# Sums of squares of the q and k heads as two float32r products, with the low parts made on GpSimd and VectorE

## The chip, the cores and the metric

The kernel runs on one core of one Trainium2 chip. Its time is the device time of one execution in microseconds (us); the median of several runs is compared. The engines are named as in the profile: PE is TensorE's matmul, PEld its weight load, DVE is VectorE, ACT is ScalarE, POOL is GpSimd, and SP issues most of the transfers.

## The reference

The reference computes two transformer blocks over 512 tokens of width 1024. The part that the change touches is in the first block, a gated DeltaNet with four heads of 128:

```
qkv = jax.nn.silu(centred_depthwise_conv(jnp.concatenate([q, k, v], axis=-1), conv_w))
q, k, v = jnp.split(qkv.astype(jnp.float32), 3, axis=-1)
q = l2_norm(q.reshape(b, s, DN_HEADS, DN_HEAD_DIM)) * (DN_HEAD_DIM ** -0.5)
k = l2_norm(k.reshape(b, s, DN_HEADS, DN_HEAD_DIM))

def l2_norm(x):
    return x * lax.rsqrt(jnp.sum(x * x, axis=-1, keepdims=True) + EPS)
```

There are eight such heads, four of q and four of k. Around them stand the input projection (`h @ w_in`), a second attention with rotary embedding in the same block, and the recurrence that uses the normed q and k.

## The kernel before

**Storage.** q and k lie with the 128 channels of a head on the partitions: `QK[:, j, :]` is head j (0 to 3 are q, 4 to 7 are k) by 512 tokens, in float32. A sum over a head's channels is thus a sum over partitions. It is made on PE by a product with a 128x128 matrix of ones, whose result holds the sum in every partition.

**Precision of the large products.** Each weight and each activation is split into a high part in float32r and a low part, and a product is three float32r products (high by high, high by low, low by high; `mm3`). A unit of weights is loaded by SP into `RAW`, ACT writes its high part `WH` (`prep`), and POOL writes the low part `WL = RAW - WH` (`prep`, 128x1024). Four buffers of each go round. In rows of the trace the high and low parts are `wh`, `wl` and `xh`, `xl`.

**Order of work.** Every engine has one queue and runs it strictly in order. One list, ORDER, is built at the top of the program by calls of `do(name, ...)`; each engine walks the list and emits its own part of every step, so a step's place in the list is its place in each queue. Waits are semaphores: `mark.up(key)` counts, `on.wait_ge(*mark.at(key))` waits. The eight PSUM banks are handed out by rings (`G.take`); whoever takes a bank waits on PE for its last reader.

**The stretch around the change.** Twelve units j = 0 to 11 of the projection give q, k and v by channel. For each, PE makes 24 products (`ch`), DVE multiplies the bank by the token's norm (`conv_rms`; rows `bank<-bank,rb`), ACT copies it with the middle tap (`conv_copy`), DVE adds the other four taps with four instructions (`conv`; rows `qk<-bank,pparams,qk`, and `vc<-...` for j of 8 and more), and ACT applies SiLU (`silu`). One step behind follows ACT's square of a finished head (`square`, into `SL8[j]`). Between these stand DVE's steps for gates and for the rotary embedding (`gate_beta`, `rope(3)` in step 2, `gate2` in step 4, `rope_k` in step 6), and POOL's weight preparations.

Then 16 pieces of a token-wise projection (`tok_pieces`, six products each; rows `bank<-wh,xh` and so on) run on PE. Behind pieces 3, 4, 5 and 6 PE makes two sums of squares each (`qsum`), from the ring of banks 6, 7, 5, 4. ACT takes the logarithm of each sum (`sl<-bank,ceps`), later the exponential of -0.5 times it, and DVE multiplies the head by the result (`qk<-qk,sl`). The sums' banks 4 and 5 were last used by `conv` 10 and `conv` 11. After that come the matrix inversions of the recurrence and the windowed attention, then the rest of both blocks.

Of the kernel before, what the change touches and what calls it, by code (L numbers as in the profile page):

```python
# [7 lines left out]
F32 = mybir.dt.float32  # L8
F32R = mybir.dt.float32r
BF16 = mybir.dt.bfloat16  # L10
ALU = mybir.AluOpType
# [186 lines left out]
def program(nc, x, xt, wflat, cfd, ppd, prd, wsd, tbd, seld, out):  # L198
# [58 lines left out]
    VT = zb("vt", [128, 4, 512], F32, 80)  # L257
    SL8 = [zb(f"sl{j}", [128, 512], F32, 72 + 2 * j) for j in range(8)]
    MIX = zb("mix", [128, 4, 1024], F32, 88)
    SWR = zb("swr", [128, 4, 640], F32, 104)  # L260
# [114 lines left out]
    def mark(name):  # L375
        marks.append(Mark(nc, name))
        return marks[-1]
# [5 lines left out]
    conv_a, conv_v, conv_s = mark("conv_a"), mark("conv_v"), mark("conv_s")  # L383
    qk_p, qk_a, qk_v = mark("qk_p"), mark("qk_a"), mark("qk_v")
    tok_p, tok_a = mark("tok_p"), mark("tok_a")
# [259 lines left out]

    G.over((6, 7, 5, 4))
    for n in tok_pieces(U_SZ, "sz"):
        if 3 <= n < 9:
            step(g1, 2)
# [488 lines left out]
    def pool_engine(e):  # L1138
# [12 lines left out]
        def prep_half(k):  # L1151
# [3 lines left out]
                w_lo.up(0 if k else "first"), 1)  # L1155

        def inv_mb(cb, d):
            W = WORK[cb]
            mb = W["MB"][d][:]
            on.wait_ge(*inv_v.at(("mb0", cb, d)))  # L1160
            e.tensor_tensor(h3(mb), h3(mb), bc4((cf("SL"), cf("SU"))[d]), ALU.mult).then_inc(inv_g.up(("mb1", cb, d)), 1)  # L1161
            if d:
                on.wait_ge(*inv_g.at(("mb1", cb, 1)))
                both = W["MB"][0][:]
                e.tensor_tensor(both, both, mb, ALU.add).then_inc(inv_g.up(("mb", cb)), 1)  # L1165
# [109 lines left out]
        def finish(tb):  # L1275
            if tb == 3:
# [3 lines left out]

        return dict(finish=finish, prep=prep, prep_half=prep_half, inv_mb=inv_mb, inv_m=inv_m, inv_mt=inv_first, inv_d=inv_d, inv_tri=inv_tri, inv_x7=inv_x7, inv_causal=inv_causal, z_gain=z_gain, swa_o=swa_o,
                    vb_first=vb_first, scan_vb=scan_vb, scan_kd=scan_kd, gm_w=gm_w, gm_sq=gm_sq, gm_gain=gm_gain, fa_norm=fa_norm, fa_low=fa_low)
# [3 lines left out]
    def scalar_engine(e):  # L1286
# [69 lines left out]
        def square(j):  # L1356
            on.wait_ge(*conv_s.at(j))
            on.wait_ge(*rope_v.at(("ss", 3) if j < 4 else "ssk"))
            act(SL8[j][:], QK[:, j, :], ACT.Square, qk_a.up(("sq", j)))

# [294 lines left out]
    def vector_engine(e):  # L1655
# [35 lines left out]
        def masks():  # L1691
# [6 lines left out]
            e.tensor_copy(IDb[:], cf("ident")).then_inc(const_set.up("id"), 1)  # L1698
            ts(HALF[:], cf("ident"), 0.5, None, ALU.mult, const_set.up("half"))
            e.memset(LNQ[:], -0.5 * math.log(128.0)).then_inc(const_set.up("lnq"), 1)  # L1700
            on.wait_ge(s_params, 32)
# [8 lines left out]
        def conv(j):  # L1710
# [3 lines left out]
            for n, i in enumerate((0, 1, 3, 4)):  # L1714
                lo, hi, sh = max(0, 2 - i), min(T, T + 2 - i), i - 2
                if n:
                    on.wait_ge(*conv_v.at((j, n)))
                stt(dst[:, lo:hi], psum[b][:, lo + sh:hi + sh], pp("dn_conv_w", j * 5 + i), dst[:, lo:hi], ALU.mult, ALU.add,
                    conv_v.up((j, n + 1)))

        def qexp(j):
# [416 lines left out]
        def finish(tb):  # L2138
# [12 lines left out]
            for n in range(tb // 3, 2):  # L2151
                c = slice(n * 512, (n + 1) * 512)
                stt(OUT[:, tb, c], H[:, tb, c], rr, GAIN[:, c], ALU.mult, ALU.mult, fin_v.up(("out", tb, n)))

        return dict(begin=begin, x_split=x_split, conv_rms=conv_rms, scale=scale, split=split, masks=masks, conv=conv, qexp=qexp, gate_dt=gate_dt, gate_beta=gate_beta, gate2=gate2, rope_tables=rope_tables, rope_sq=rope_sq,
                    rope_root=rope_root, rope=rope, rope_keys=rope_keys, rope_k=rope_k, rope_t=rope_t, inv_decay=inv_decay, inv_mb=inv_mb, inv_q=inv_q, inv_m=inv_m,
# [7 lines left out]
    def tensor_engine(e):  # L2164
# [147 lines left out]
        def qsum(j):  # L2312
            p = bank(("qsum", j))
            on.wait_ge(s_const, 16)
            on.wait_ge(*qk_a.at(("sq", j)))
            mm(p[:, :], cf("ones"), SL8[j][:], True, True).then_inc(qk_p.up(j), 1)

# [359 lines left out]
```

## Time and profile before

| | |
|---|---|
| median of 3 runs | 923.9 us (923.84 to 924.92) |
| the profiled execution's own time | 923.39 us |
| its span, first to last instruction | 921.6 us |
| PE busy | 906.2 us, 98% of the span |
| DVE busy | 481.8 us, 52% |
| ACT busy | 457.4 us, 50% |
| POOL busy | 464.1 us, 50% |
| mean granted TensorE clock | 0.999 |

Busy time is an average over stages with different limits. Matmuls are pipelined, so the duration of a PE row (0.39 us for 128x512) is longer than the distance between the starts of two, and it is the distance that counts in a sum. A float32 product appears as two PE instructions. Names in rows are out<-in, with buffer numbers left out: `sl` is any of the eight `SL8`.

### The profile page before, as it was taken

The page shows a single profiled execution, that of the slowest core. Times are in us where ns is not written, and L with a number is a line of the kernel's source. Part 1 is how long each engine was busy: PE and PEld are TensorE (multiplying, and loading weights), DVE is VectorE, ACT ScalarE, POOL GpSimd, SP SyncE. Part 2 cuts the span into 40 slices and gives each one's busy share as a digit, 9 for nine tenths or more (in the row PEclk, how much of TensorE's full clock was granted, in tenths as well). Part 3 has the DMA queues.
Part 4 walks back from the last instruction along what each step waited for, and adds up shares of the span by engine and source line. Part 5 has one row for each costly group of instructions (what it writes and reads, how often), then busy time and mean ns, then how long its engine had stood idle before and what let it go on. Part 6 is the DMA issues. An engine that isn't in the chain of part 4 may idle for free.

```text
span 921.6 us, 11979 instructions
## 1 busy us (share of the span) xinstructions
PE 906.2 (98%) x4752; PEld 763.7 (83%) x4752; DVE 481.8 (52%) x814; ACT 457.4 (50%) x817; POOL 464.1 (50%) x262
## 2 busy tenths in 40 slices
PE   9999999999999999999999999999999999999997
PEld 6988868899999888788777889888888888888885
DVE  4679836898857443533654434333333334654434
ACT  6666587576546444447557245333343433433223
POOL 4453432987566433456786426444444444344440
PEclk9999999999999999999999999999999999999999
DMA  9522310000022714332221214233222233232202
GB/s 344 191 91 91 97 42 1 1 1 2 2 92 68 267 46 137 115 92 70 75 86 46 97 60 132 101 104 101 92 92 92 91 96 110 73 133 93 91 23 92
DMA packets 25303, 83.63 MB, mean 91 GB/s; under 512 B 3008, under 2 KB 3264, under 8 KB 25120
## 3 DMA queue, kind: packets, MB, share of 16 engines
q1 hardware_dynamic: 24240, 81.49, 26.4%
q10 hardware_dynamic: 1008, 1.38, 0.4%
q8 instruction: 38, 0.62, 0.3%
q14 instruction: 17, 0.14, 0.0%
HBM read 78.66 MB, written 2.10 MB: 88 GB/s over the span
## 4 chain that ended last, share of the span: by engine, by line
PE 81%; DVE 9%; POOL 5%; ACT 3%; DMA 1%; issue 1%; SPq 0%; DVEq 0%; ACTq 0%
PE bank L2168 78%; PE bank L2176 3%; DVE qk L1665 2%; DVE vc L1665 1%; POOL mb L1161 1%; POOL wl L1149 1%; DVE r L1659 1%; ACT L1290 1%; DMA xt<-in_xt 1%; POOL mb L1165 1%; POOL p L1251 1%; POOL dd L1171 1%; DVE bank L1659 0%; ACT vc L1290 0%; ACT xh L1290 0%
## 5 line engine op out<-in xcount | busy, mean ns | idle before, releaser
L1149 POOL TENSOR_TENSOR wl<-raw,wh 128x1024 fp32r<-128x1024 f32 (+1 forms) x129 | 310.3, 2410 | 364.0 <-ACT wh L1290 364.0
L2168 PE MATMUL bank<-xh,wh 128*128 128x512 f32 (+1 forms) x536 | 206.8, 386 | 0.0
L2168 PE MATMUL bank<-xl,wh 128*128 128x512 f32 (+1 forms) x536 | 205.2, 383 | 0.0
L2168 PE MATMUL bank<-xh,wl 128*128 128x512 f32 (+1 forms) x528 | 202.2, 383 | 0.0
L1290 ACT ACTIVATE wh<-raw 128x1024 fp32r<-128x1024 f32 (+2 forms) x132 | 136.0, 1035 | 123.9 <-PE bank L2168 117.8
L2168 PE MATMUL bank<-wh,xh 128*128 128x512 f32 (+1 forms) x352 | 140.5, 399 | 0.8 <-POOL wl L1149 0.4
L2168 PE MATMUL bank<-wh,xl 128*128 128x512 f32 (+1 forms) x352 | 134.5, 382 | 0.0
L2168 PE MATMUL bank<-wl,xh 128*128 128x512 f32 (+1 forms) x352 | 134.1, 381 | 0.0
L2168 PEld LDWEIGHTS bank<-xh,wh 128*128 128x128 f32 x536 | 100.8, 188 | 19.3 <-issue 0.2
L2168 PEld LDWEIGHTS bank<-xl,wh 128*128 128x128 f32 x536 | 100.8, 188 | 19.2
L2168 PEld LDWEIGHTS bank<-xh,wl 128*128 128x128 f32 x528 | 99.2, 188 | 19.6
L2168 PEld LDWEIGHTS bank<-wh,xh 128*128 128x128 f32 x352 | 66.3, 188 | 15.5 <-POOL wl L1154 1.7
L1659 DVE TENSOR_TENSOR al<-ac,ah 128x512 fp32r<-128x512 f32 x22 | 53.6, 2450 | 45.8 <-ACT ah L1290 45.8
L2168 PEld LDWEIGHTS bank<-wh,xl 128*128 128x128 f32 x352 | 66.1, 188 | 13.0
L2168 PEld LDWEIGHTS bank<-wl,xh 128*128 128x128 f32 x352 | 66.4, 189 | 11.8 <-issue 1.0
L1665 DVE SCALAR_TENSOR_TENSOR ta<-bank,pparams,ta 128x510 f32<-128x510 f32 (+1 forms) x44 | 32.9, 749 | 74.1 <-ACT ta L1290 73.3
L2168 PE MATMUL bank<-wh,ah 128*128 128x512 f32 x176 | 68.5, 389 | 0.0
L2168 PE MATMUL bank<-wl,ah 128*128 128x512 f32 x176 | 68.5, 389 | 0.0
L2168 PE MATMUL bank<-wh,al 128*128 128x512 f32 x176 | 68.5, 389 | 0.0
L1665 DVE SCALAR_TENSOR_TENSOR tgg<-bank,pparams,tgg 128x510 f32<-128x510 f32 (+1 forms) x44 | 33.0, 749 | 62.4 <-ACT tgg L1290 61.6
L1290 ACT ACTIVATE tgg<-bank,pparams 128x512 f32<-128x512 f32 x22 | 17.2, 781 | 78.8 <-PE bank L2168 78.8
L1251 POOL TENSOR_SCALAR p<-p,dn 128x512 f32<-128x512 f32 (+3 forms) x32 | 34.8, 1089 | 16.8 <-DVE dn L2079 16.7
(271 smaller groups left out, 1424.7 us busy)
## 6 DMA issues: line engine op xcount, KB each, us to landing
raw<-in_wflat SPq DMA_DIRECT2D x126, 512.0 KB, 3.5
xt<-in_xt SPq DMA_DIRECT2D x8, 256.0 KB, 4.4
h<-in_x SPq DMA_DIRECT2D x4, 512.0 KB, 8.1
h<-in_x SPq DMA_DIRECT2D x1, 2048.0 KB, 8.3
gain<-in_pr SPq DMA_DIRECT2D x3, 512.0 KB, 5.0
consts<-in_cf SPq DMA_DIRECT2D x1, 1088.0 KB, 10.5
raw<-in_wflat SPq DMA_DIRECT2D x4, 272.0 KB, 11.0
kh<-kh SPq DMA_DIRECT2D x8, 128.0 KB, 2.3
```

The costliest lines, as they stand in the source:

```text
L1149: e.tensor_tensor(WL[u % NS][:, 0:n], RAW[u % NS][:, 0:n], WH[u % NS][:, 0:n].bitcast(F32), ALU.subtract).then_inc(w_lo.up(u), 1)
L1161: e.tensor_tensor(h3(mb), h3(mb), bc4((cf("SL"), cf("SU"))[d]), ALU.mult).then_inc(inv_g.up(("mb1", cb, d)), 1)
L1165: e.tensor_tensor(both, both, mb, ALU.add).then_inc(inv_g.up(("mb", cb)), 1)
L1171: e.tensor_tensor(h3(W["DD"][:, lower(d)]), h3(raw(cb)), bc4(cf("LM", d)), ALU.mult).then_inc(inv_g.up(("dd", cb, 0, d)), 1)
L1251: e.tensor_scalar(p, p, DN2[:, qb, h:h + 1], None, ALU.mult).then_inc(fa_g.up(n), 1)
L1290: return e.activation(out_, in_, f, **k).then_inc(up, 1)
L1659: return e.tensor_tensor(out_, a, b, op).then_inc(up, 1)
L1665: return e.scalar_tensor_tensor(out_, a, s, b, op0, op1).then_inc(up, 1)
L2168: return e.matmul(o, l, r_, start=start, stop=stop, skip_group_check=part)
L2176: return e.transpose(o, in_, cf("ident")[0:in_.shape[0], 0:in_.shape[0]])
```

## The change

1. POOL gets a step `square`: it computes head squared in float32 into `SL8[j]`, at the place in the list where ACT has its square.
2. ACT's square now writes float32r into a new tile `SQH[j]`: the high part.
3. DVE gets a step `sq_low`: `SQL[j] = SL8[j] - SQH[j]`, float32r, in the place of `SL8[j]`. The eight stand behind `conv` 11.
4. PE's `qsum` makes two float32r products with a float32r matrix of ones (`ONES`, made once by DVE), high then low, in place of one float32 product.
5. The ring of banks for the sums is 6, 7, 4, 5.

```
-    G.over((6, 7, 5, 4))
+    G.over((6, 7, 4, 5))
     for n in tok_pieces(U_SZ, "sz"):
+        if n < 4:
+            do("sq_low", 2 * n)
+            do("sq_low", 2 * n + 1)
         if 3 <= n < 9:
             step(g1, 2)
...
+        def square(j):
+            on.wait_ge(*conv_s.at(j))
+            on.wait_ge(*rope_v.at(("ss", 3) if j < 4 else "ssk"))
+            e.tensor_tensor(SL8[j][:], QK[:, j, :], QK[:, j, :], ALU.mult).then_inc(qk_g.up(j), 1)
...
-            act(SL8[j][:], QK[:, j, :], ACT.Square, qk_a.up(("sq", j)))
+            act(SQH[j][:], QK[:, j, :], ACT.Square, qk_a.up(("sq", j)))
...
+            ts(ONES[:], cf("ones"), 1.0, None, ALU.mult, const_set.up("ones"))
...
+        def sq_low(j):
+            on.wait_ge(*qk_a.at(("sq", j)))
+            on.wait_ge(*qk_g.at(j))
+            tt(SQL[j][:], SL8[j][:], SQH[j][:].bitcast(F32), ALU.subtract, sq_v.up(j))
...
+            on.wait_ge(*const_set.at("ones"))
             on.wait_ge(*qk_a.at(("sq", j)))
-            mm(p[:, :], cf("ones"), SL8[j][:], True, True).then_inc(qk_p.up(j), 1)
+            mm(p[:, :], ONES[:], SQH[j][:], True, False)
+            on.wait_ge(*sq_v.at(j))
+            mm(p[:, :], ONES[:], SQL[j][:], False, True).then_inc(qk_p.up(j), 1)
```

On PE, behind piece 3 of the token-wise projection, before (the first and the second pair of sums, six products of piece 4 between them):

```order
L2168 MATMUL bank6<-sl0_79,consts_61 128x512 [waits qk_a,s_const,gate_v]
L2168 MATMUL bank7<-sl1_80,consts_61 128x512 [waits qk_a]
...
L2168 MATMUL bank5<-sl2_81,consts_61 128x512 [waits qk_a,conv_v]
L2168 MATMUL bank4<-sl3_82,consts_61 128x512 [waits qk_a]
```

The same place on PE in the changed kernel:

```order
L2186 MATMUL bank6<-sqh0_87,onesr_95 128x512 [waits const_set,qk_a,s_const,gate_v]
L2186 MATMUL bank6<-sql0_96,onesr_95 128x512 [waits sq_v]
L2186 MATMUL bank7<-sqh1_88,onesr_95 128x512 [waits qk_a]
L2186 MATMUL bank7<-sql1_97,onesr_95 128x512 [waits sq_v]
...
L2186 MATMUL bank4<-sqh2_89,onesr_95 128x512 [waits qk_a,conv_v]
L2186 MATMUL bank4<-sql2_98,onesr_95 128x512 [waits sq_v]
L2186 MATMUL bank5<-sqh3_90,onesr_95 128x512 [waits qk_a,conv_v]
```

Every sum now has two products, and the second of them waits for a result of DVE (`sq_v`), in the first pair too.

On DVE, the end of the twelfth unit's taps and what stands behind it in the changed kernel:

```order
L1677 SCALAR_TENSOR_TENSOR vc_76<-bank5,pparams_62,vc_76 128x510 [waits conv_v]
L1671 TENSOR_TENSOR sql0_96<-sl0_79,sqh0_87 128x512 [waits qk_g,qk_a]
L1671 TENSOR_TENSOR sql1_97<-sl1_80,sqh1_88 128x512 [waits qk_g,qk_a]
L1671 TENSOR_TENSOR sql2_98<-sl2_81,sqh2_89 128x512 [waits qk_g,qk_a]
```

Before, the last tap of `vc` was followed directly by `qk<-qk,sl`; now the eight subtractions stand between the two, and none stands ahead of the taps.

On POOL, the weight preparations of steps 2 to 6, in the changed kernel:

```order
L1156 TENSOR_TENSOR wl1_58<-raw1_50,wh1_54 128x1024 [waits w_hi]
L1167 TENSOR_TENSOR sl0_79<-qk_75 128x512 [waits rope_v,conv_s]
L1156 TENSOR_TENSOR wl2_59<-raw2_51,wh2_55 128x1024 [waits w_hi]
L1167 TENSOR_TENSOR sl1_80<-qk_75 128x512 [waits conv_s]
L1156 TENSOR_TENSOR wl3_60<-raw3_52,wh3_56 128x1024 [waits w_hi]
L1167 TENSOR_TENSOR sl2_81<-qk_75 128x512 [waits conv_s]
L1156 TENSOR_TENSOR wl0_57<-raw0_49,wh0_53 128x1024 [waits w_hi]
L1167 TENSOR_TENSOR sl3_82<-qk_75 128x512 [waits conv_s]
L1156 TENSOR_TENSOR wl1_58<-raw1_50,wh1_54 128x1024 [waits w_hi]
L1167 TENSOR_TENSOR sl4_83<-qk_75 128x512 [waits rope_v,conv_s]
L1156 TENSOR_TENSOR wl2_59<-raw2_51,wh2_55 128x1024 [waits w_hi]
L1167 TENSOR_TENSOR sl5_84<-qk_75 128x512 [waits conv_s]
```

Before, only the `wl` rows stood there; one square has been put behind each of eight preparations (two more follow those shown).

## Rows read from the trace of the kernel before

**Rows 1.** Busy by stretch: PE, PEld, DVE, ACT, POOL, then granted clock, DMA share, GB/s.
```profile
60.00:108.60 48.60, 48.60 (x219) 40.29 (x218) 44.93 (x66) 28.38 (x41) 20.99 (x9) 1.00 0.26 90
108.60:127.30 18.70, 18.17 (x66) 12.02 (x65) 7.44 (x11) 11.93 (x17) 5.82 (x3) 1.00 0.21 68
```
**Rows 2.** The chain in order of time, 90 to 320 us: start, duration, engine.
```profile
117.82 21.83 PE bank L2168 x84
```
**Rows 3.** Timeline of PE, 103 to 128 us: start, duration, engine, instruction [idle before].
```profile
103.14 0.39 PE L2168 MATMUL bank<-xh,wh 128*128 128x512 f32 x1
...
113.79 0.39 PE L2168 MATMUL bank<-wh,xl 128*128 128x512 f32 x1
114.02 1.88 PE L2168 MATMUL bank<-sl,consts 128*128 128x512 f32 x4
...
117.82 1.98 PE L2168 MATMUL bank<-sl,consts 128*128 128x512 f32 x4 [0.53 <-DVE vc L1665]
...
121.02 1.88 PE L2168 MATMUL bank<-sl,consts 128*128 128x512 f32 x4
...
127.22 0.40 PE L2168 MATMUL bank<-wh,xh 128*128 128x512 f32 x1
```
**Rows 4.** Timeline of DVE, 129 to 135 us.
```profile
129.75 5.17 DVE L1659 TENSOR_TENSOR qk<-qk,sl 128x512 f32<-128x512 f32 x8 [11.98 <-ACT sl L1290]
```
**Rows 5.** Timeline of ACT, 118 to 120 us.
```profile
118.45 1.28 ACT L1290 ACT_TABLE_LOAD   x1
```
**Rows 6.** Tile `vsq`: shortest, median and longest ns of POOL's square of a tile.
```profile
L1268 POOL TENSOR_TENSOR vsq<-vg x4: 1035/1043/1062, 434.1 to 450.7; 128x512 f32<-128x512 f32 x4
```
**Rows 7.** Timelines of POOL and of DVE, 62 to 71 us.
```profile
62.42 2.40 POOL L1149 TENSOR_TENSOR wl<-raw,wh 128x1024 fp32r<-128x1024 f32 x1 [4.58 <-ACT wh L1290]
66.41 2.50 POOL L1149 TENSOR_TENSOR wl<-raw,wh 128x1024 fp32r<-128x1024 f32 x1 [1.59 <-ACT wh L1290]
...
62.71 2.14 DVE L1662 TENSOR_SCALAR beta<-beta 128x32 f32<-128x32 f32 x1
...
65.80 0.26 DVE L1665 SCALAR_TENSOR_TENSOR gg<-spa,ea 128x16 f32<-128x16 f32 x2
...
66.70 3.43 DVE L1659 TENSOR_TENSOR r<-swr,turnq 128x512 f32<-128x512 f32 x3
```
**Rows 8.** Timelines of POOL (86 to 102 us) and of DVE (80 to 94 us).
```profile
86.85 2.41 POOL L1149 TENSOR_TENSOR wl<-raw,wh 128x1024 fp32r<-128x1024 f32 x1 [2.38 <-ACT wh L1290]
90.46 2.67 POOL L1149 TENSOR_TENSOR wl<-raw,wh 128x1024 fp32r<-128x1024 f32 x1 [1.19 <-ACT wh L1290]
99.96 2.42 POOL L1149 TENSOR_TENSOR wl<-raw,wh 128x1024 fp32r<-128x1024 f32 x1 [6.83 <-ACT wh L1290]
...
80.83 0.19 DVE L1659 TENSOR_TENSOR nbeg<-nbeta,eg 128x32 f32<-128x32 f32 x1 [1.61 <-ACT eg L1290]
...
88.39 1.42 DVE L1659 TENSOR_TENSOR swr<-swr,ssk 128x512 f32<-128x512 f32 x1
89.85 3.56 DVE L1659 TENSOR_TENSOR r<-swr,turnk 128x512 f32<-128x512 f32 x3
```
**Rows 9.** Timelines of POOL and of DVE, 162 to 166 us.
```profile
162.40 1.30 POOL L1161 TENSOR_TENSOR mb<-mb,consts 128x512 f32<-128x512 f32 x1
163.65 1.75 POOL L1210 TENSOR_TENSOR ds<-ds,consts 128x512 f32<-128x512 f32 x1
...
163.16 1.09 DVE L1659 TENSOR_TENSOR mb<-ee,nbeta 128x512 f32<-128x512 f32 x1
```
**Rows 10.** Busy by stretch at the end of the span, columns as in rows 1.
```profile
914.00:916.00 2.00, 1.49 (x7) 0.91 (x5) 0.77 (x2) 0.72 (x2) 1.29 (x1) 1.00 0.66 246
...
918.00:919.00 1.00, 0.00 (x0) 0.00 (x0) 0.47 (x1) 0.50 (x1) 0.00 (x0) 0.93 0.00 0
919.00:920.00 1.00, 0.00 (x0) 0.00 (x0) 0.00 (x0) 0.00 (x0) 0.00 (x0) 0.50 0.66 252
```
**Rows 11.** Timeline of PE, 0 to 12 us: the program's first products.
```profile
1.47 5.49 PE L2168 MATMUL bank<-zero 128*128 128x512 f32 x6 [1.47 <-DVE zero L1669]
```

More of the change, by code:

```diff
@@ L258, in program @@
     SL8 = [zb(f"sl{j}", [128, 512], F32, 72 + 2 * j) for j in range(8)]
+    SQH = [zb(f"sqh{j}", [128, 512], F32R, 32 + 2 * j) for j in range(8)]
+    ONES = sb("onesr", [128, 128], F32R, small_at[0])
+    small_at[0] += 0.5
+    SQL = [zb(f"sql{j}", [128, 512], F32R, 72 + 2 * j) for j in range(8)]
     MIX = zb("mix", [128, 4, 1024], F32, 88)
@@ L383, in program @@
     conv_a, conv_v, conv_s = mark("conv_a"), mark("conv_v"), mark("conv_s")
-    qk_p, qk_a, qk_v = mark("qk_p"), mark("qk_a"), mark("qk_v")
+    qk_p, qk_a, qk_v, qk_g, sq_v = mark("qk_p"), mark("qk_a"), mark("qk_v"), mark("qk_g"), mark("sq_v")
     tok_p, tok_a = mark("tok_p"), mark("tok_a")
@@ L1279, in finish @@
                 e.tensor_tensor(HG[:], H[:, 3, 0:512], GAIN[:, 0:512], ALU.mult).then_inc(fin_g.up("hg"), 1)
-        return dict(finish=finish, prep=prep, prep_half=prep_half, inv_mb=inv_mb, inv_m=inv_m, inv_mt=inv_first, inv_d=inv_d, inv_tri=inv_tri, inv_x7=inv_x7, inv_causal=inv_causal, z_gain=z_gain, swa_o=swa_o,
+        return dict(finish=finish, square=square, prep=prep, prep_half=prep_half, inv_mb=inv_mb, inv_m=inv_m, inv_mt=inv_first, inv_d=inv_d, inv_tri=inv_tri, inv_x7=inv_x7, inv_causal=inv_causal, z_gain=z_gain, swa_o=swa_o,
                     vb_first=vb_first, scan_vb=scan_vb, scan_kd=scan_kd, gm_w=gm_w, gm_sq=gm_sq, gm_gain=gm_gain, fa_norm=fa_norm, fa_low=fa_low)
@@ L2153, in finish @@
                 stt(OUT[:, tb, c], H[:, tb, c], rr, GAIN[:, c], ALU.mult, ALU.mult, fin_v.up(("out", tb, n)))
-        return dict(begin=begin, x_split=x_split, conv_rms=conv_rms, scale=scale, split=split, masks=masks, conv=conv, qexp=qexp, gate_dt=gate_dt, gate_beta=gate_beta, gate2=gate2, rope_tables=rope_tables, rope_sq=rope_sq,
+        return dict(begin=begin, x_split=x_split, conv_rms=conv_rms, scale=scale, split=split, masks=masks, conv=conv, sq_low=sq_low, qexp=qexp, gate_dt=gate_dt, gate_beta=gate_beta, gate2=gate2, rope_tables=rope_tables, rope_sq=rope_sq,
                     rope_root=rope_root, rope=rope, rope_keys=rope_keys, rope_k=rope_k, rope_t=rope_t, inv_decay=inv_decay, inv_mb=inv_mb, inv_q=inv_q, inv_m=inv_m,
```

## The prediction

> **What bounds the kernel now.** I read the stretches first, then the chain in order of time, then the timelines of the engines on both sides of the change. From 60 to 108.6 us PE is never idle, but DVE is busy for 44.93 of 48.60 us [rows 1]: two engines run side by side there, and busy shares do not say which one is late. The chain of work does. Through the units 2 to 11 it lies on DVE (taps, gates, rotary embedding), with short turns to ACT, up to the last tap of `conv` 11. At 117.82 it passes to PE, which then holds it for 21.83 us without a gap [rows 2]. So PE, though busy, has slack ahead of 117.8: it starts unit 11 at 103.14 and is at the first pair of sums at 114.02 [rows 3], almost 4 us before DVE is through. It stands still once only, 0.53 us in front of the second pair, for bank 5 and its reader `conv` 11 [rows 3]. **Whatever delays DVE between 62 and 118 us delays the end by as much, and whatever PE must await from DVE behind `conv` 11 is on the path.** The change does both.
>
> **The products.** Forty-eight products start between 103.14 and 114.02, the last at 113.79, so one float32r product costs 10.65/47 = 0.227 us [rows 3]. From 121.02 to 127.22 there are two pairs of float32 sums and twelve products: 6.20 us, less 12 x 0.227, leaves 1.74 us a pair [rows 3]. A pair in the new form is four float32r products, 0.91 us. Four pairs save 4 x 0.83 = 3.3 us of PE work, and the new order of banks would let the first of the second pair go ahead of `conv` 11. No row shows float32r products with a matrix of ones, but only the values differ.
>
> The Trainium skill (TensorE: Matmul & The Clock Gate, Back-to-back issue gap) gives 131 ns for a sustained 512-column product in a stream with weight loads. By that figure a new pair would cost 0.52 us as an estimate, and the three pairs behind the first wait would end 1.2 us earlier. The rows show 0.227 us in just such a stream, and I go by them.
>
> **The wait that the change adds.** The low product of the first sum waits for `sq_low` 0, and DVE reaches `sq_low` only behind `conv` 11. Before, ACT's squares had been made long ahead. The nearest row to one subtraction is DVE's `qk<-qk,sl`, of the same size and also with two SBUF inputs: 8 in 5.17 us, so 0.65 each, 0.60 where they follow each other closely [rows 4]. With `conv` 11 ending at 117.8 (PE starts at 117.82, released by it [rows 3]), the first low part is there at 118.45 and the second at 119.05. PE then does the last product of pair 1 (0.23), six products (1.36), and three times a pair and six products (0.91 + 1.36 = 2.27): 119.07 + 0.23 + 1.36 + 6.80 = 127.46. Before, the same point is 127.22 [rows 3]. **The whole saving is thus used up, +0.24 us.** The later low parts come every 0.60 us against 0.91 us for two sums and 1.36 us between pairs, so only the first pair waits. Queued behind PE's wait are all later products; all of them wait. ACT does not add to it: its table load ends at 119.73 [rows 5], when the first two sums are done.
>
> **The squares on POOL.** Eight more instructions. The nearest row is POOL's own square of a 128x512 tile, 1.043 us [rows 6]; POOL's products of two tiles of that size take 1.30 us [rows 9], which is the upper bound. POOL itself is only 43% busy there [rows 1], and a square by itself delays no weights that matter. But the rows show that a VectorE instruction with SBUF inputs cannot run during a POOL instruction: `beta`, 128x32, takes 2.14 us from 62.71 until POOL's 62.42 + 2.40 is over; `swr<-swr,ssk` takes 1.42 instead of 0.69; three `r` take 3.43 and 3.56 us around POOL's other preparations [rows 7, 8]. The taps, which read PSUM, keep their length. And the turn goes to whoever waits when an instruction ends: `mb<-ee,nbeta` on DVE gets in between two POOL instructions, and the second of these takes 1.75 us where its like takes 1.30 [rows 9].
>
> With that I go through DVE's queue.
> - *62 to 71 us (`gate_beta`, `rope(3)`).* Square 0 stands directly behind the preparation that ends at 64.82, so `nbeta` waits until about 65.87, 0.6 us late. Then `gg`, at 65.80 before, comes after 66.41, when the next preparation holds the port, and it and `swr` (0.6 us) no longer fit in ahead of it. They run from 68.85 on. Square 1, ready behind that preparation, takes one more turn of 1.04 us. Sum: 0.6 to 0.9 us for the order, plus 1.04: **1.6 to 1.9 us** later.
> - *78 us (`gate2`).* Square 2 can delay `ngc` by a turn, but DVE waits 1.61 us for ACT right there [rows 8]. Nothing.
> - *88 to 94 us (`rope_k`).* Four `swr`/`r` steps and the sum `swr` stand against two preparations [rows 8]. Now POOL has preparation, square 4, preparation, square 5 without a gap, as the heads 4 and 5 are finished one step earlier. Each square gets one turn between DVE's instructions: **2 x 1.04 = 2.0 us** (2.1, less what the two overlap between instructions).
> - Squares 3, 6 and 7 fall beside taps. Nothing.
>
> Sum 3.5 to 3.9 us; I take 3.8. At the upper price of 1.30 a square it would be 4.6, at none of it 0. The same squares made at the rate that the Trainium skill gives for GpSimd's `tensor_tensor` (GPSIMD Engine Reference, Elementwise — side-by-side cycle accounting), about 2.6 cycles an element, would be an estimate of 1.11 us each and 4.0 us in all.
>
> Behind 94 us DVE's chain has no slack, so `conv` 11 ends at 121.6. PE's slack takes a part: the weights of unit 11 are ready at 99.96 + 2.42 = 102.38 [rows 8], only 0.76 us ahead of their use, and ACT's preparation follows DVE. So PE stands 3.0 us in front of unit 11, arrives at pair 1 at 117.1, and waits there from 117.3 to 122.2. That costs nothing more, since it is waiting for the same DVE.
>
> **Small parts.** DVE's `ONES` is one 128x128 instruction in the opening stretch, where PE's products bind; at most 0.2 us. The new addresses cost nothing. The subtractions use DVE's idle 11.98 us [rows 4].
>
> **Sum.** 0.24 + 3.8 = +4.0 us on a span of 921.6 us. The profiled execution took 923.39 us and would take 927.4; the median of the runs is 0.5 us above it. **Forecast 928.0 us.** Behind 127 us everything hangs on PE's piece stream [rows 2], so I see no slack that gives a part back.
>
> **Rivals.**
> 1. *The clock falls during the long wait.* Before, PE is busy for 48.60 of 48.60 and 18.17 of 18.70 us here, with the clock at 1.00 [rows 1]. At the end of the span its last products end at 915.5, and the granted clock falls to 0.50 (1.2 GHz) inside 918 to 919 [rows 10]. The wait from 117.3 to 122.2 is longer than that. At the start, PE works at the low level from 1.47 to about 7 us: three float32 products take 5.49 us, 1.83 each [rows 11] against 0.87 above. If the clock falls and comes back after a similar time, some 5.5 us at half speed lose about 2.7 us: 930.7 us. For it: the length. Against it: the wait could be 1 us shorter if DVE loses less. The Trainium skill (TensorE: Matmul & The Clock Gate, What's actually happening) has the chip look at the activity in windows that run on regardless of the kernel, so a wait of this length would sometimes be caught and sometimes not, in the runs of one kernel; no row before can show this.
> 2. *The squares pass beside DVE* (another turn order, or a square that is not kept out). Then only the +0.24 remains: 924.1 us, with part of the loss up to 925.7.
> 3. *Faster.* The wait at pair 1 would have to be gone: then 3.3 us and the stall of about 0.7 us (0.53 in the row, and the restart) are saved, 919.9 us. It decides itself by whether `sq_low` 0 is done when PE arrives at 114.2; it stands behind `conv` 11 in DVE's queue, so DVE would have to end its taps 4 us earlier. The change takes nothing from DVE ahead of that point. A weaker form: the delay of PE is caught up further on, where the inversions keep ACT, DVE and POOL busy. But what starts those is PE's own stream.
>
> **How the numbers follow.** Forecast mechanism, clock kept: 0.45. With the clock falling: 0.27. Little or no loss on DVE (924.1 to 925.7): 0.13. A part of the loss (925.8 to 926.8): 0.08. Faster: 0.05. Above 932: 0.02. The range leaves out the faster case and the lower half of the case without loss below, and the last above: 925.0 to 932.0. By itself the forecast mechanism spans 926.9 to 928.8. A difference of 0.2%, 1.8 us, is about what a measurement of this kernel tells from none; slower by more is 0.45 + 0.27 + 0.08 + 0.02 and a little of the third case, 0.83; within it 0.12; faster 0.05.
>
> **What would show each step.** In the timeline of PE: sums as pairs of float32r products 0.227 us apart, a wait for DVE's `sql` in front of the first low product, of 4 to 5 us, and none at the other pairs. On DVE: `nbeta` or `gg` near 66 us and the `r` near 90 us stretched further, the last tap at about 121.6, first `sql` directly behind it. On POOL: squares of 1.04 us. In the stretches: a clock below 1.00 behind 121 us or not. The prediction is wrong if the last tap still ends near 118, if PE does not stop at pair 1, or if the piece stream behind the sums does not set the next stage's start.

## The result

The changed kernel takes 928.5 us in the median of five runs (927.29 to 930.51), the kernel before, timed beside it, 924.92 us: a ratio of 1.0045, interval 1.0032 to 1.0058. It is slower by 0.45%. Its profiled execution took 930.51 us, with a span of 928.7 us, against 923.39 us and 921.6 us.

The chain of work in order of time (start, duration, what), around the change. It answers to [rows 2].

```profile
67.54 4.29 DVE r L1671 x3
...
91.55 5.14 DVE r L1671 x3
...
121.69 23.21 PE bank L2186 x93
```

As before, DVE holds the chain up to the last tap and then PE takes it over, but at 121.69 and no longer at 117.82. The timeline of PE (start, duration, engine, instruction, idle before); it answers to [rows 3].

```profile
105.74 0.47 PE L2186 MATMUL bank<-xh,wh 128*128 128x512 f32 x1 [2.01 <-POOL wl L1156]
...
116.74 0.40 PE L2186 MATMUL bank<-sqh,onesr 128*128 128x512 f32 x1
...
121.69 0.50 PE L2186 MATMUL bank<-sql,onesr 128*128 128x512 f32 x1 [4.54 <-DVE sql L1671]
...
122.29 0.75 PE L2186 MATMUL bank<-sql,onesr 128*128 128x512 f32 x1
...
127.89 0.39 PE L2186 MATMUL bank<-sqh,onesr 128*128 128x512 f32 x1
...
128.58 0.40 PE L2186 MATMUL bank<-sql,onesr 128*128 128x512 f32 x1
```

The reader sees the sums as float32r products, 0.23 us apart in the third pair (127.89 to 128.58), and one wait of 4.54 us in front of the very first low product. The second low product takes 0.75 us. Why, the stretches of PE tell (busy, then granted clock):

```profile
120.00:122.00 2.00, 0.31 (x1) 1.00 0.00 0
122.00:124.00 2.00, 2.00 (x6) 0.59 0.00 0
124.00:126.00 2.00, 2.00 (x6) 0.55 0.00 0
126.00:128.00 2.00, 2.00 (x10) 1.00 0.00 0
```

TensorE comes back from the wait and drops to its lower level, 1.2 GHz, for 3.4 us; in that time products start 0.43 us apart instead of 0.23. Before, the clock was 1.00 throughout here [rows 1]. What keeps DVE late is in its own timeline and POOL's; they answer to [rows 7, 8, 4].

```profile
63.15 2.15 DVE L1674 TENSOR_SCALAR beta<-beta 128x32 f32<-128x32 f32 x1
65.33 0.35 DVE L1758 RECIPROCAL beta<-beta 128x32 f32<-128x32 f32 x1
65.72 0.58 DVE L1674 TENSOR_SCALAR nbeta<-beta 128x32 f32<-128x32 f32 x1
...
67.54 4.28 DVE L1671 TENSOR_TENSOR r<-swr,turnq 128x512 f32<-128x512 f32 x3
...
91.55 5.13 DVE L1671 TENSOR_TENSOR r<-swr,turnk 128x512 f32<-128x512 f32 x3
...
117.93 3.10 DVE L1677 SCALAR_TENSOR_TENSOR vc<-bank,pparams,vc 128x510 f32<-128x510 f32 x4 [0.76 <-ACT vc L1302]
120.95 4.89 DVE L1671 TENSOR_TENSOR sql<-sl,sqh 128x512 fp32r<-128x512 f32 x8
```

And POOL's:

```profile
65.22 1.04 POOL L1167 TENSOR_TENSOR sl<-qk 128x512 f32<-128x512 f32 x1
66.85 2.92 POOL L1156 TENSOR_TENSOR wl<-raw,wh 128x1024 fp32r<-128x1024 f32 x1 [0.58 <-ACT wh L1302]
69.72 1.49 POOL L1167 TENSOR_TENSOR sl<-qk 128x512 f32<-128x512 f32 x1
...
90.93 1.49 POOL L1167 TENSOR_TENSOR sl<-qk 128x512 f32<-128x512 f32 x1
92.38 2.84 POOL L1156 TENSOR_TENSOR wl<-raw,wh 128x1024 fp32r<-128x1024 f32 x1
95.18 1.22 POOL L1167 TENSOR_TENSOR sl<-qk 128x512 f32<-128x512 f32 x1
```

The three `r` that took 3.43 us take 4.28, those that took 3.56 take 5.13, with POOL's squares beside them; the squares take 1.04 us by themselves, as in [rows 6], and up to 1.49 where DVE has a turn first. The last tap ends at about 120.95, and the eight `sql` follow at 0.60 us each.

**Where the 7.1 us of span lie.** I compare the start of each TensorE product with that of the same product before. The shift is 0.41 us already at 13.4 us, in the opening, where the kernels hardly differ; other kernels' executions have it too, and it is not the change's. Behind the last pair of sums it is 5.28 us; below, "the end of the sums" is always the same product, the second behind the last pair (126.07 us before). DVE's own start in this stretch is 0.44 us late at 62.71 us (63.15). It loses 1.26 us more by 72 us and another 1.57 by 97 us, 2.83 together, and the last taps start 3.27 us late. With 0.24 for the pairs and 1.7 for the clock (the products of the 3.4 us started at about half the rate) that makes 0.44 + 2.83 + 0.24 + 1.7 = 5.2 of the 5.28 us. A last step, 1.7 us, comes at 195 us, far from the change. There DVE adds the sinks of the attention to its maxima, a tile of 128x8 (`es`). First its row, then POOL's beside it:

```profile
198.34 3.03 DVE L1671 TENSOR_TENSOR es<-rparams,mx 128x8 f32<-128x8 f32 x1
```
```profile
196.33 5.02 POOL L1200 TENSOR_TENSOR mp<-ds,consts 128x512 f32<-128x512 f32 x4
```

In the kernel before the same instruction, with the same four `mp` beside it, took 0.54 us. The experiments show that this step belongs to neither kernel.

The granted clock of the whole execution is known for the other timed runs too. It was 0.998 in the profiled execution, with its 3.4 us at the lower level, and 0.995 to 0.997 in the other four. No profiled execution on record in which the clock fell only at the very end of the span has less than 0.998. So the clock very probably fell in those four as well.

### The profile page after: what moved, and what is told of

Read it like the earlier page. It is cut to its first block, busy times and chain, and to the rows that moved or that the text cites. A ratio compares the mean times of both kernels' runs of the same rounds, so it can differ in the third digit from the quotient of the medians.

```text
span 928.7 us, 12007 instructions
## 1 busy us (share of the span) xinstructions
PE 905.0 (97%) x4752; PEld 764.7 (82%) x4752; DVE 493.7 (53%) x823; ACT 457.8 (49%) x817; POOL 474.0 (51%) x270
## 4 chain that ended last, share of the span: by engine, by line
PE 79%; DVE 11%; POOL 5%; ACT 3%; issue 1%; DMA 1%; SPq 0%; DVEq 0%; ACTq 0%
PE bank L2186 76%; PE bank L2194 3%; DVE qk L1677 2%; DVE vc L1677 1%; DVE r L1671 1%; POOL mb L1173 1%; POOL wl L1156 1%; DVE dt L1671 1%; ACT L1302 1%; DMA xt<-in_xt 1%; POOL mb L1177 1%; POOL p L1263 1%; POOL dd L1183 1%; DVE bank L1671 0%; ACT vc L1302 0%
```

## The experiments

Each kernel was timed in five rounds beside the kernel before. "Shift" is always the start of TensorE's products against the profiled execution of the kernel before, and holds the opening's part where nothing else is said: 0.2 to 0.5 us, and -0.2 us in experiment 6.

**1. The squares out of DVE's way.** POOL makes them while DVE reads PSUM.

```
         if 2 <= j <= 9:
             do("square", j - 2)
+        for i in {5: (0, 1), 7: (2, 3, 4, 5, 6), 8: (7,)}.get(j, ()):
+            do("square_low", i)
```
(`square` is ACT's alone now, `square_low` POOL's; from head 2 on it also waits for the end of `rope_k`.)

> The change, with POOL's squares moved to where DVE runs only taps that read PSUM: two in step 5, five in step 7 behind the last swr of the rotated keys, one in step 8. Everything else as changed. My account (DVE kept off its SBUF inputs by POOL's squares costs 2.85 us): the last tap of conv 11 ends 2.5 to 3 us earlier than in the changed kernel (at 117.8 to 118.2 of the span), the wait at the first pair stays at 4 us or so, and the time is 2.5 to 3 us below the changed kernel's, that is about +0.3 to +2 us against the kernel before (0.24 and what a fall of the clock costs). Rival (the squares are not what delays DVE): last tap still near 121, time still +3.5 to +4.5 us.

Measured: 927.39 us (926.36 to 928.17), ratio 1.0032 [1.002, 1.0044]; the profiled execution 926.36 us. DVE's delay is gone: no wait for `wl`, and `conv` 11 ends at 118.0. The low product is there at 118.66, but the clock falls here too. PE's timeline:

```profile
118.66 0.80 PE L2190 MATMUL bank<-sql,onesr 128*128 128x512 f32 x1 [4.03 <-DVE sql L1675]
```

Its stretches (busy, then granted clock):

```profile
116.00:118.00 2.00, 0.00 (x0) 0.72 0.33 133
118.00:120.00 2.00, 1.34 (x3) 0.50 0.00 0
120.00:122.00 2.00, 2.00 (x6) 0.50 0.00 0
122.00:124.00 2.00, 2.00 (x7) 0.58 0.00 0
```

The shift at the end of the sums is 2.86 us: 0.2 of the opening, 0.24, and about 2.5 for 5 us of products at 1.2 GHz. So the delay of DVE is one cause, and the wait for `sq_low` behind `conv` 11 is a second one that stays by itself and brings the third, the clock. The median falls by only 1.1 us, less than the 2.8 us that DVE regains. The six runs had a granted clock of 0.994 to 0.997, the changed kernel's 0.995 to 0.998, so the clock took a larger part here; the profiled execution is the fastest of the six.

**2. PE kept at work during the wait.** Eighteen discarded products, results of no use, stand between the first high and the first low product.

```
             mm(p[:, :], ONES[:], SQH[j][:], True, False)
+            if j == 0:
+                spare = bank(("qsum", 1))
+                for _ in range(18):
+                    mm(spare[:, :], XH[:, 0, 0:128], WH[0][:, 0:512], True, True)
```

> The change, with 18 products whose result is thrown away on PE behind the first high product, in a bank of a later sum, so that PE works through most of its long wait. My account (the granted clock fell to 0.5 because of that wait and cost 1.7 us): the clock stays at 1.00 around 120 us, and the time is about 1.7 us below the changed kernel's, +2 to +2.5 us against the kernel before. Rival (the fall of the clock is hidden by other waits, or was a chance of the one profiled run): time as the changed kernel's, +3.6 to +4, with the clock kept.

Measured: 928.88 us (928.07 to 929.58), ratio 1.0044 [1.0031, 1.0056]. PE's timeline, and a stretch (busy, then granted clock):

```profile
117.04 4.24 PE L2186 MATMUL bank<-wh,xh 128*128 128x512 f32 x18
121.74 0.50 PE L2186 MATMUL bank<-sql,onesr 128*128 128x512 f32 x1 [0.46 <-DVE sql L1671]
```
```profile
120.00:122.00 2.00, 1.54 (x7) 1.00 0.00 0
```

The clock stays at 1.00 in every stretch from 118 to 126 us, PE's last wait is 0.46 us, and the shift at the end of the sums is 3.85 us, 1.43 less than in the changed kernel. But `es` at 196.90 us took 3.01 us here too, and in the timed runs nothing of the gain is to be seen, although their granted clock was 0.997 to 0.999 against the changed kernel's 0.995 to 0.998. The clock's price is thus shown in the trace alone, not in the medians, and what hides it there is open.

**3. The high part taken twice.** The kernel before, with two float32r products of the high part for each sum, in the new ring, and neither squares on POOL nor `sq_low`. It leaves out the low part, and its sums are twice as large.

> The kernel before with ACT's square in float32r, two float32r products of the high part per sum, the new order of banks, no squares on POOL and no subtractions. Leaves out the low part and adds the high part twice, so the sums are twice as large. My account (the products save 0.83 us a pair, the order of banks some of the stall of 0.7): PE stands in front of conv 11's bank until 117.8, and the end of the sums comes at 124.2 in place of 127.2: 3.0 us faster than before. Rival (the saving does not reach the end, because another engine binds behind the sums): within 1 us of before.

Measured: 923.73 us (922.16 to 925.4, 11 runs), ratio 0.9985 [0.9975, 0.9995], profiled 922.62 us. A pair takes 0.93 us against the 0.91 of the estimate, so the saving of 3.3 us of PE's work is real. But at the end of the sums the shift is -1.37 us (-1.85 without the opening's part), not -3.0. The expectation missed; the list of PE's waits in the stretch says where it went (total, times, longest):

```profile
PE bank L2172 <- DVE vc L1668: 0.9, 1, 0.9
PE bank L2172 <- ACT sl L1293: 0.6, 1, 0.6
```

PE runs ahead and stands, first for the bank of `conv` 11, then at the third pair for bank 6, which ACT frees only by its first logarithm: behind `conv` 11 ACT must apply SiLU, load a table and then take the logarithm.

**4. The order of banks alone.** The kernel before with the ring 6, 7, 4, 5.

> The kernel before with the new order of banks only. My account: the first sum of the second pair (0.87 us) goes ahead of conv 11's end, the wait of 0.53 us and its restart go, 0.7 us faster than before. Rival: no difference, as DVE binds anyway.

Measured: 924.48 us (923.17 to 926.4, 11 runs), ratio 1.0001 [0.9992, 1.0011]. In the trace the wait at the second pair is gone, and from 118.35 to 120.79 us the shift is -0.34 us, 0.8 less than in the opening. Half of this goes at the third pair, which starts at 120.97 us and not at 120.69, where PE's stream would have it: as in experiment 3 it takes bank 6, and ACT reads that bank only from 120.23 on. About 0.4 us are left up to 195 us (a shift of 0.06 to 0.00 against the opening's 0.46). Then 1.7 us are lost: DVE's timelines of the kernel before (first) and of this one (second):

```profile
193.01 0.54 DVE L1659 TENSOR_TENSOR es<-rparams,mx 128x8 f32<-128x8 f32 x1
```
```profile
193.01 3.03 DVE L1659 TENSOR_TENSOR es<-rparams,mx 128x8 f32<-128x8 f32 x1
```

Both begin at 193.01, with POOL's four `mp` from 191.0 to 196.0 beside them. In the one execution DVE gets in between two of them, in the other it is passed over until the last is done. This is a difference of the execution and not of the change. It fits the times of the kernel before: of its 100 timed runs beside the changed kernel and these experiments 40 lie between 923.17 and 924.09 us, 60 between 924.81 and 927.26, and none between. The top of the upper group goes with a lower clock: of the 95 runs beside the experiments eleven have a granted clock of 0.996, and they are the eleven slowest, 926.20 to 927.26 us; all others have 0.998 or more.

**5 and 6. That small step later.** `es` and ACT's exponential of it are made one piece later, in the changed kernel and in the kernel before (DVE's part; ACT's likewise).

```
-            if h == 7:
-                on.wait_ge(*swa_v.at(("mx", n)))
-                tt(ES[:, qb, :], pr("swa_sinks"), MX[:, qb, :], ALU.add, swa_v.up(("es", qb)))
+            for m in range(n - 1, n + 1):
+                if m >= 0 and m % 8 == 7 and (m < n or n == 31):
+                    on.wait_ge(*swa_v.at(("mx", m)))
+                    tt(ES[:, m // 8, :], pr("swa_sinks"), MX[:, m // 8, :], ALU.add, swa_v.up(("es", m // 8)))
```

> The changed kernel with one small step moved: the sum of sinks and maxima (es, 128x8) of a block of attention is made one piece later, and ACT's exp of it too, so that VectorE's small operation at 198 us no longer stands beside GpSimd's row of four mp operations. Theory: that operation took 3.03 us because GpSimd held the port over several operations; moved, it takes under 1.4 us, the shift of TensorE's products against the kernel before stays at the value that it has at the end of the sums (5.3 us with the clock's fall, 3.6 without), and the timed runs lie at 926.0 to 927.5 with a spread under 1 us. Rival: the 1.7 us at 195 to 200 us come from another wait (ACT or TensorE), and come back at the same place: median 928.5.

> The same move in the kernel before. Theory: the timed runs of the kernel before fall into two groups (923.2 to 923.9 and 924.8 to 926.6) by whether the small operation meets GpSimd's row; with it moved, only the lower group is left: median 923.2 to 923.9, ratio 0.998 to 1.000, and the difference between this run and the one with the changed kernel is the change's own price: 2.85 for VectorE's delay, 0.24 for the wait, 0 or 1.7 for the clock, so 2.6 to 4.8 us. Rival: two groups stay, as the step has another cause.

Measured: 928.46 us (927.06 to 929.85) and 924.46 us (the median of eleven runs, one of them of 3230.82 us; the others 923.33 to 925.34), ratios 1.0032 [1.0022, 1.0042] and 0.9987 [0.9977, 0.9997]. In both traces the first `es` took 1.12 to 1.14 us and no step is left at 195 us (the shift of experiment 6 at its end is -0.07 us). But the spread did not fall under 1 us, and the median of experiment 6 is 924.5 us, not 923.2 to 923.9. So the theory holds in the profiled executions and is not confirmed by the times: something more spreads them, and it is not the clock, which was granted at 0.998 or more in all of experiment 6's runs. In experiment 8, which moves the step too, `es` even took 2.40 us: a later place is no sure way out. The two kernels differ by 4.0 us in the medians, inside the 2.6 to 4.8 expected for the change's own price.

The trace of experiment 5 has something else, PE's stretches at the preceding wait:

```profile
104.00:106.00 2.00, 0.34 (x2) 1.00 0.00 0
106.00:108.00 2.00, 2.00 (x8) 0.76 0.64 217
108.00:110.00 2.00, 2.00 (x6) 0.50 0.11 45
```

PE has stood for `wl` for 2.02 us, as in the changed kernel, and here the clock falls behind this wait; in the executions of the changed kernel and of experiments 8 and 10 it stayed at 1.00 behind the same wait. It fell a second time during the wait of 2.94 us for `sql`, at 120.7 us, before PE was back at 121.61. The shift at the end of the sums is 6.24 us.

**7 and 8. The sums three pieces later.** `if 6 <= n < 12` in place of `if 3 <= n < 9`, so that PE asks for the sums eighteen products later, 4.1 us at 0.227 each (the expectation of experiment 8 says 3.3); experiment 7 with the squares as in experiment 1, experiment 8 with the squares left where the change has them, both with the sinks' step moved.

> The changed kernel with the sinks' step moved, GpSimd's squares placed where VectorE reads PSUM or a bank, and the sums of squares put three pieces later in TensorE's order (pairs 0 to 5 between pieces 6 and 11 of the step instead of 3 and 8). Theory: VectorE is not held up, sq_low of the first head is there before TensorE asks for it, nothing waits, and the clock stays at 1.00: the products save 3.3 us and the kernel before's own wait of 0.53 us goes as well; 3.3 to 3.9 us under the kernel before with the sinks moved, 919.5 to 920.5. Rival 1: ACT's logarithm behind the last convolution frees the first bank late and holds part of it back, as with the high part taken twice: 921 to 922. Rival 2: the later place in the order itself costs what follows the sums (transposes, rope): 923 or more.

> As the run above, but GpSimd's squares stay where the change has them. Theory: VectorE ends the last convolution 2.85 us late, at about 120.7, TensorE has three pieces more to do before it asks (some 3.3 us of products), so its wait shrinks from 4.54 us to 1 us or less, the clock stays at 1.00, and the saving of 3.3 us is there against a delay that now lies partly beside TensorE: 920.5 to 923.5. If 2.85 us of VectorE's delay still reach the end, the rival that the delay and not the wait costs: 923 to 924.

Measured: 925.47 us (923.84 to 926.91, 11 runs), ratio 1.0003 [0.9993, 1.0013], and 929.54 us (the median of seven runs, one of them of 1833.76 us; the others 927.78 to 929.73), ratio 1.0037 [1.0023, 1.0051]. Both are slower than the theory had it. In experiment 7 the long wait is gone, the clock is 1.00, and the shift is -2.17 us once all sums are made, from 127.5 us on. Then it goes back to +0.46 at 138 us. PE's timeline, then ACT's and DVE's:

```profile
138.59 0.50 PE L2192 MATMUL bank<-wh,xh 128*128 128x512 f32 x1 [2.46 <-ACT mix L1306]
```
```profile
137.84 2.42 ACT L1306 ACTIVATE mix<-bank,rs 128x512 f32<-128x512 f32 x4
```
```profile
118.07 9.32 DVE L1676 TENSOR_TENSOR sql<-sl,sqh 128x512 fp32r<-128x512 f32 x8
```

PE needs a bank that ACT empties by `mix`, and `mix` stands in ACT's queue behind SiLU, three table loads, eight logarithms, eight exponentials and weight splits. Before, `mix` began at 136.85 and with the 0.75 us that lie between the start of `mix` and PE's product here, PE could have gone on at 137.60, while it came at 138.12. So 0.5 us is all that PE can come forward as long as ACT does not. Here ACT is itself 1 us later, for the last logarithms must wait for the last sums; and these were late because POOL's `wl` preparations, two of them at 119.85 and 123.39 us, now fall beside the eight `sql`, which take 9.32 us instead of 4.89. Experiment 8 adds to this the 2.0 us for `wl` and the delay of DVE. Behind its wait for `mix`, 2.45 us, the clock fell too (0.50 from 142 to 144 us) and took 1.6 us, which the wait of 2.46 us at the same place in experiment 7 did not bring; with 1.2 us more at `es` it ends at +6.22 us. Rival 2 of the expectation came about. Rival 1 did not: no sum of experiment 7 waited for a bank, and PE's waits there were for `sql` (0.67 us) and for `mix`.

**9 to 11. Three low parts early.** In front of the taps of `conv` 9, 10 and 11 DVE waits 0.76 us for ACT's copy. Experiment 9 makes one `sql` in each of these gaps, and has the squares as in experiment 1.

```
+        if j >= 9:
+            do("sq_low", j - 9)
...
-            do("sq_low", 2 * n)
-            do("sq_low", 2 * n + 1)
+        for i in (2 * n, 2 * n + 1):
+            if 3 <= i < 8:
+                do("sq_low", i)
```

> The changed kernel with GpSimd's squares out of VectorE's way and the first three low parts (sql of heads 0 to 2) made in VectorE's gaps of 0.76 us in front of the taps of convolutions 9, 10 and 11, where it waits for ACT's vc. Theory: TensorE's first low products find their operands, the wait for sql (4.0 us without this step) falls under 0.5 us and the clock stays at 1.00 between 112 and 130 us; the products are 3.3 us shorter and TensorE's old wait of 0.53 goes, but ACT (silu, table load, eight logarithms, exponentials, copies to mix) has only 1.1 us of idle time between 117.8 and 139 us in the kernel before and becomes the bound, so TensorE waits for ACT's sl or mix and only 1.0 to 1.7 us are left at the end: profiled execution 922.0 to 922.8 when the small operation at 195 us is short, ratio 0.998 to 0.999. Rival: ACT is no bound, the whole 3.3 to 3.8 us reach the end: 919.5 to 920.0, ratio 0.996.

Measured: 923.63 us (922.6 to 926.66, 12 runs), ratio 0.9991 [0.9981, 1.0001]; profiled 922.99 us. The first low product no longer waits, the clock stays at 1.00, and the shift at the end is -0.42 us, the opening's 0.4 included. ACT's timeline:

```profile
118.75 0.63 ACT L1308 ACTIVATE vc<-vc 128x512 f32<-128x512 f32 x1 [3.17 <-DVE vc L1683]
119.40 1.28 ACT L1308 ACT_TABLE_LOAD   x1
120.70 2.42 ACT L1308 ACTIVATE sl<-bank,ceps 128x512 f32<-128x512 f32 x4
...
123.94 2.44 ACT L1308 ACTIVATE sl<-bank,ceps 128x512 f32<-128x512 f32 x4
...
136.50 2.43 ACT L1308 ACTIVATE mix<-bank,rs 128x512 f32<-128x512 f32 x4
```
PE's one longer wait is 1.4 us, for the bank of `conv` 11. From SiLU to `mix` ACT now has no gap: 17.75 us, against 19.05 before, which had 1.08 us of waiting for PE. So of the 3.3 us saved on PE about 1.3 us can reach `mix`, and 0.95 us of this is lost again, as SiLU starts at 118.75 instead of 117.80: 0.24 stem from before 104 us, the rest from the `sql` before `conv` 9. That one took 1.65 us, for a `wl` (103.81 to 106.21) ran beside it. DVE's timeline:

```profile
105.12 1.65 DVE L1677 TENSOR_TENSOR sql<-sl,sqh 128x512 fp32r<-128x512 f32 x1
```

Experiment 10 has the three early low parts, with the squares left where the change has them.

> The changed kernel with the three early low parts alone; GpSimd's squares stay where the change has them. Theory: VectorE still ends convolution 11 some 2.85 us late (about 120.6 to 121), ACT's silu and the logarithms start that much later, and TensorE waits for a bank or for convolution 11 instead of for sql; with ACT as the bound behind it, nearly the whole 2.85 us less the 1.1 of ACT's idle time reach the end: shift at the end +1.5 to +3.0 against the kernel before, plus what the clock costs where the wait is over 2 us: 925.5 to 928. Rival: the delay mattered only through the wait for sql, which is gone: 923 or less.

Measured: 927.0 us (926.1 to 927.78, 11 runs), ratio 1.0022 [1.0013, 1.0031]. The shift behind the sums, at 142 us, is 2.52 us against -0.38 in experiment 9: **the squares' place costs 2.9 us**, with the clock at 1.00 in both profiled executions and nothing else different up to there; the medians differ by 3.4 us. The timed runs are less clean: seven of the eleven here have a granted clock of 0.996 or 0.997, in experiment 9 three of twelve. Those seven are no slower than the other four, so the difference of the medians is not the clock's. The rival, that the delay mattered only through the wait for `sql`, is out.

Experiment 11 was to move one weight split out of ACT's row.

```
     do("conv", 11)
+    w_ahead(U_SZ + 2)
     do("silu", 11)
```

> As the first run of this batch, and one weight split (wh of the third unit of the projection beside the sums, 1.05 us on ACT) taken out of the row of logarithms and put ahead of the silu behind convolution 11, where ACT is idle for 3.2 us. Theory: ACT is the bound between 118 and 139 us, so its chain and the products behind mix come 0.9 to 1.05 us earlier than in the first run of this batch: 921.0 to 921.8 profiled. Rival 1: ACT is no bound: no difference. Rival 2: GpSimd's low part of that unit (2.4 us), which then starts at about 116 us, keeps VectorE off SBUF at the sql behind convolution 11 and gives the gain back: no difference or up to 1 us more.

That split had been issued already at this point of the list, so ACT's order is that of experiment 9, row for row, and the run is a second measurement of it: 923.18 us (922.71 to 925.91, 12 runs), ratio 0.9983 [0.9974, 0.9992]. What an earlier split is worth was not tried.

**12. Two low parts early,** without the one that met the `wl`.

> As the run with three low parts early, with only two of them in VectorE's gaps (heads 0 and 1, ahead of the taps of convolutions 10 and 11); that of head 2 is made behind convolution 11 again. Theory: in the run with three, the one ahead of convolution 9 stood beside GpSimd's low part of weights and took 1.65 us instead of 0.68, which delayed the taps by about 0.5 us (5 ends at 118.6 instead of 118.1); without it convolution 11 ends 0.4 to 0.5 us earlier, and since head 2's pair waits for the bank of convolution 11 in any case, ACT's row of logarithms, and with it everything behind, comes 0.4 to 0.5 us earlier: shift at the end -0.8 to -1.0 against the kernel before in an execution with the short operation at 195 us, profiled 922.3 to 922.7, ratio 0.997 to 0.999. Rival: head 2's low part, now made after convolution 11, makes TensorE wait for it and ACT's second logarithm late: no gain over the run with three.

Measured: 923.49 us (921.83 to 925.65, 12 runs), ratio 0.9989 [0.9978, 1.0001]. `conv` 11 ends at 118.1, 0.5 us earlier than in experiment 9, as expected. But PE, in front of the third low product, waited 1.70 us for `sql`. It came back at the full clock, and 1.3 us later, at work, it fell to 1.2 GHz, as its timeline and its stretches (busy, granted clock) show:

```profile
118.84 0.50 PE L2192 MATMUL bank<-sql,onesr 128*128 128x512 f32 x1 [1.70 <-DVE sql L1677]
```
```profile
118.00:120.00 2.00, 1.16 (x4) 1.00 0.00 0
120.00:122.00 2.00, 2.00 (x6) 0.54 0.00 0
122.00:124.00 2.00, 2.00 (x7) 0.60 0.00 0
```

ACT then waited 1.03 us for the last sums, and the shift at the end is +0.28 us, 0.7 more than with three, though the fastest runs, 921.83 us, are the lowest of all. The versions of experiments 9, 11 and 12 are 5 us faster than the changed kernel, and at 0.9983 to 0.9991 no more than level with the kernel before or just under it.

## Why the prediction was right, and where not

**What bounds the kernel: right.** Whatever delays DVE between 62 and 118 us delays the end: experiments 9 and 10, which differ only in the squares' place, are 2.9 us apart in the trace.

**The products: right.** 0.91 us a pair was the estimate, 0.93 us experiment 3 measured. That the saving of 3.3 us would come through whole if nothing waited was not right: experiments 3 and 7 show ACT's row from SiLU to `mix` as the next bound, and the prediction's faster rival of 919.9 us overlooked it. Nothing reached it; the best profiled execution is that of experiment 3, at 922.62 us, the best timed run one of experiment 12, at 921.83 us.

**The wait behind `conv` 11: right,** in place and size. 4.54 us of wait were expected to be 4 to 5, and the balance of +0.24 us closes the sums of the changed kernel and of experiment 1 to within 0.1 us. Only the first pair waits.

**The squares on POOL: mechanism right, size too large.** The term was 3.8 us and measured 2.83. In the first stretch it was 1.26 us in place of 1.6 to 1.9. The step that failed is that `gg` and `swr` would no longer fit in ahead of the next preparation: they did, `swr` by 0.03 us (66.82 against 66.85), and held the preparation up instead, which took 2.92 us where it had taken 2.50. In the second stretch it was 1.57 us in place of 2.0 for two full turns; why two squares cost less than two turns there no experiment took apart. `conv` 11 ended at 121.0, not 121.6, and PE stood 2.01 us for unit 11, not 3.0.

**The rule of turns: not general.** That an instruction with SBUF inputs cannot run during one of POOL's was too wide: `RECIPROCAL` kept its 0.35 us beside a square. The rule of turns was read from one place [rows 9] and served for the order near 66 and 90 us. At 193.01 us the same instruction, beside the same four of POOL, got its turn in one execution and none in another.

**The clock: the rival came about** beside the forecast mechanism, in the profiled execution by its trace and very probably in the other four runs, by their granted clock of 0.995 to 0.997. The sum had put this term at nothing. In the trace the clock stayed low for 3.4 us and took 1.7 us, not 5.5 and 2.7 us. The 5.5 us had been read from the length of the span's first products, beside which the stretches show a granted clock of 1.00; behind a wait in mid-span the clock was low for 3.4 us or, in experiments 1 and 5, for 6.8. In the Trainium skill (TensorE: Matmul & The Clock Gate, What's actually happening) the chip's view of activity runs on regardless of the kernel, so that one and the same wait is caught or not. The traces agree: behind the 2.0 us for `wl` the clock fell in experiment 5 and not in the changed kernel, and behind the 2.5 us for `mix` in experiment 8 and not in experiment 7. In experiment 12 it fell behind a wait of 1.70 us.

**The sum.** 928.0 us was forecast and 928.5 measured, 0.05% off, partly by errors that cancel: 0.97 us too much for DVE's delay, nothing for the clock (1.7 us in the profiled execution), nothing for the event at 195 us (1.7 us there). Against the profiled execution alone, 930.51 us, the 927.4 of the mechanism is 3.1 us short; 1.7 + 1.7 + 0.44 less 0.97 make 2.9 of it. The median fits the same terms without the step at 195 us: 923.39 + 0.44 + 2.83 + 0.24 + 1.7 = 928.6 us. The forecast came as near by 3.8 in place of 2.83 us for DVE, no clock, and the 0.5 us that it added for the median: the number is in part luck. Whether `es` was short in those four runs no trace shows. The claim that nothing behind 127 us gives a part back held for the changed kernel (5.28 us at the end of the sums, 5.33 at 194 us). It is not general: where PE comes early, ACT's row up to `mix` takes a part, 0.5 us in experiment 9 (-0.93 to -0.42) and 3.1 in experiment 7 (-2.17 to +0.95).

## What to carry to other kernels

Work saved on one engine is worth no more than the slack of whichever engine is next at that place: here 3.3 us of TensorE's time shrank to about one, since ScalarE's row of table loads, logarithms and copies had just 0.5 us to spare. A result put at the end of a busy engine's queue costs its consumer the whole distance; look for gaps in that queue where it can be made early, and place GpSimd's own instructions where VectorE reads PSUM. Both together took this change from 928.5 to 923.6 us; the clear place for the squares alone reached 927.4, the three early low parts alone 927.0. A wait of some 2 us on TensorE can have a price beyond its length, since the products behind it may run at half the clock, 1.6 to 1.7 us for 3.4 us of it here.

## What the runs showed of the hardware

- A VectorE instruction of 128x8 with SBUF inputs took 0.54 us in one execution and 3.03 us in another, started at the same 193.01 us beside the same row of four GpSimd instructions. The chip has no fixed turn between the two engines that these traces would show.
- TensorE's clock fell to the 1.2 GHz level in executions with waits of 1.70 us (experiment 12), 2.02 and 2.94 (experiment 5), 2.45 (experiment 8), 4.03 (experiment 1) and 4.54 us (the changed kernel). It did not fall behind 2.01 us in the changed kernel, 2.1 us in experiment 10 or 2.46 us in experiment 7. In experiments 1 and 5 it had fallen before the wait for `sql` was over, in experiment 12 only 1.3 us after PE was back at work.
- Four taps that read PSUM took 3.09 us from 86.85 us, as before, with a square of POOL from 86.12 to 87.17 beside them. `RECIPROCAL`, with one SBUF input of 128x32, took 0.35 us while a square ran (65.22 to 66.26), and `nbeta` directly behind it 0.58, up to the square's end.
